# mLSTM gates as three f32r products of split parts, computed between the query/key blocks and the V projection

## Chip, core and metric

The kernel runs on one core of one Trainium2 chip. The metric is the time of one execution in microseconds (us) on the device. TensorE (PE in the profile) multiplies matrices, VectorE (DVE) and ScalarE (ACT) work on elements and may read PSUM, GpSimd (POOL) works on elements in SBUF alone, and SyncE (SP) issues most transfers from memory.

## What is computed

The reference is a network of two stacks with 512 tokens and 1024 channels: feed-forward layers, an attention layer, an mLSTM layer, and two convolutional and state-space mixers. The change lies in the mLSTM layer, which begins as follows (cut to what matters):

```python
proj = xn @ w_in                       # 1024 x (4 * 1024 + 2 * 8)
qk, v, o, gates = split(proj, [2048, 3072, 4096])
qk = silu(causal_depthwise_conv(qk, conv_w))          # width 4
q, k = split(qk, 2)
gates = gates + b_gates
i_pre, f_pre = gates[..., :8], gates[..., 8:]         # 8 heads each
...
bc = cumsum(log_sigmoid(f_pre))
m_t = maximum(bc + m_prev, max_s(bc_t - bc_s + i_s))  # running maximum
p = (q @ k.T / sqrt(128)) * exp(bc_t - bc_s + i_s - m_t)
hid = (p @ v + ...) / maximum(abs(sum(p) + ...), exp(-m_t))
```

The kernel treats all 512 tokens as one chunk, so that the running sum and the running maximum are two scans along a row of 512 for each of the 8 heads.

## The kernel before

**Split products.** The weights stream in blocks of 128 x 1024 (512 KB). A ring of four slots holds them: `raw` as loaded, `wh` the part rounded to f32r, `wl` the rest. SyncE issues the load of block b once block b-4 has been multiplied (`blocks_done`). ScalarE makes `wh` by a copy (`high_part`, L357), GpSimd makes `wl` by a subtraction (`low_part`, L365), and TensorE then runs 24 matmuls of 512 columns for the block (`block_mm`, L1624 to L1626): for each of 8 slices of the inner dimension `wh*xh`, `wl*xh` and `wh*xl`, where `xh` and `xl` are the two parts of the layer's input, split from `hf`.

**The query and key blocks** (section `mlstm.qk`, 16 blocks, numbered 0 to 15 here). `linear` takes the first three together as the input arrives (`first_three`, L1683 to L1688), then block 3, then loops over the other twelve. Each block ends in one of four PSUM banks, `lin[0]` to `lin[3]`. VectorE applies the convolution of width 4 to it in four instructions (L949 and L953), which frees the bank (`tiles_freed`), and ScalarE applies Silu into SBUF (L876). ScalarE's order in `conv_out` is fixed: Silu of tile m, then `high_part` of the block that goes in as number m+4, then Silu of tile m+1.

**The gates.** Behind the first three blocks, through the parameter `amid` of `linear`, TensorE runs `gates_tensor` (L781): 16 matmuls in plain f32, with weights of 8 columns (`wg`), into banks 4 and 5, on the unsplit input `hf`. They show as 32 records in the trace. VectorE then waits for them (`g_pe`) and runs the chain of gates in rows of 8 x 512, from L927 to L940, with ScalarE doing Abs, Exp, Ln and later Exp between its steps (L864 to L870, handed over by `g_vec` and `g_act`). All of this is written ahead of the first convolution in VectorE's order and ahead of the first Silu in ScalarE's. The convolution also writes to `hf`, which the gates' matmuls read.

**After block 15** TensorE transposes the two rows of gates (`gate_columns_tensor`, 8 small matmuls, L789 and L793) and starts the V projection (`token_major("mlstm.v")`, 8 blocks V0 to V7 in two halves of four, L1717 to L1719). A half waits until its four banks are free; ScalarE copies them out after each half (L886), behind the high parts of blocks V3 to V6. Then come the output gate (`mlstm.o`, 8 blocks) and the attention-like part over the heads, which reads the chain's results first at its start.

## Time and profile before

| what | value |
|---|---|
| median of 3 runs | 2794.43 us (2792.47 to 2794.62) |
| the profiled execution's own time | 2798.81 us |
| its span, first to last instruction | 2797.0 us |
| TensorE busy | 2591.9 us, 93% of the span |
| weight loads busy | 2081.1 us, 74% |
| GpSimd, ScalarE, VectorE busy | 1293.9, 1003.4 and 983.9 us |
| mean granted TensorE clock | 0.944 of full |

A busy time sums the time in which an engine had an instruction under way. A matmul's record is longer than its step: they overlap, so the distance between two starts is what one costs. The granted clock is the share of TensorE's full 2.4 GHz that the chip allowed in a stretch; it has two levels, 2.4 and 1.2 GHz, so that a mean between 0.5 and 1 is a mixture.

### The profile page before, as it was taken

How to read it: one execution, taken by the hardware profiler on the slowest of the kernel's cores; microseconds unless marked ns; L12 is line 12 of the kernel's file. 1: busy time of each engine (PE TensorE's matmuls, PEld its weight loads, DVE VectorE, ACT ScalarE, POOL GpSimd, SP SyncE). 2: the span in 40 equal slices, each digit the busy share in tenths (PEclk: the TensorE clock that was granted, in tenths of full speed). 3: DMA queues.
4: the chain of work that ended last, by engine and by line, in shares of the span. 5: the costliest groups of instructions: out<-in, count | busy, mean ns of one | idle time of the engine just before them, and what ended most of it. 6: DMA issues, size and time to landing. Idle time of an engine off the chain costs nothing. (4 is left out here: it accounts for less than half of the span.)

```text
span 2797.0 us, 31691 instructions
## 1 busy us (share of the span) xinstructions
PE 2591.9 (93%) x11348; PEld 2081.1 (74%) x11348; DVE 983.9 (35%) x1541; ACT 1003.4 (36%) x1351; POOL 1293.9 (46%) x683
## 2 busy tenths in 40 slices
PE   7999999899999999999999799989999986988787
PEld 5888878655788888888886676778888875766656
DVE  2222330044522211422213521634224169214973
ACT  4333333266533332433332323434333332234442
POOL 4555544300455554555543333136555453246843
PEclk9999989999999999999998899889999988998888
DMA  3233433200132333232331122022333322221211
GB/s 120 97 97 111 129 98 98 83 1 1 60 105 95 94 104 105 76 97 97 98 105 68 60 83 75 1 75 83 97 97 98 105 75 76 81 75 61 67 52 61
DMA packets 69332, 228.35 MB, mean 82 GB/s; under 512 B 8803, under 2 KB 13283, under 8 KB 69132
## 3 DMA queue, kind: packets, MB, share of 16 engines
q1 hardware_dynamic: 63456, 218.63, 24.4%
q10 hardware_dynamic: 4956, 5.61, 0.7%
q0 software_dynamic: 848, 3.15, 0.3%
q8 instruction: 46, 0.75, 0.1%
q14 instruction: 26, 0.21, 0.0%
HBM read 222.75 MB, written 6.84 MB: 82 GB/s over the span
## 5 line engine op out<-in xcount | busy, mean ns | idle before, releaser
L365 POOL TENSOR_TENSOR wl_sb<-raw_sb,wh_sb 128x1024 fp32r<-128x1024 f32 x401 | 971.2, 2425 | 1102.8 <-ACT wh_sb L357 1100.4
L1624 PE MATMUL banks<-xh_sb,wh_sb 128*128 128x512 f32 x2064 | 818.7, 397 | 77.0 <-POOL wl_sb L365 60.2
L1625 PE MATMUL banks<-xh_sb,wl_sb 128*128 128x512 f32 x2064 | 813.2, 394 | 0.0
L1626 PE MATMUL banks<-xl_sb,wh_sb 128*128 128x512 f32 x2064 | 812.5, 394 | 0.0
L357 ACT ACTIVATE wh_sb<-raw_sb 128x1024 fp32r<-128x1024 f32 x401 | 423.9, 1059 | 809.2 <-DMA raw_sb<-weights 805.6
L1624 PEld LDWEIGHTS banks<-xh_sb,wh_sb 128*128 128x128 f32 x2064 | 393.8, 191 | 168.9 <-issue 57.5
L1626 PEld LDWEIGHTS banks<-xl_sb,wh_sb 128*128 128x128 f32 x2064 | 393.6, 191 | 83.6
L1625 PEld LDWEIGHTS banks<-xh_sb,wl_sb 128*128 128x128 f32 x2064 | 394.6, 191 | 81.7
L1624 PE MATMUL banks<-hh_sb,wh_sb 128*128 128x512 f32 x704 | 273.9, 389 | 0.0
L1625 PE MATMUL banks<-hh_sb,wl_sb 128*128 128x512 f32 x704 | 273.9, 389 | 0.0
L1626 PE MATMUL banks<-hl_sb,wh_sb 128*128 128x512 f32 x704 | 273.9, 389 | 0.0
L2015 DVE TENSOR_TENSOR hf_sb<-banks,rstd_sb 128x512 f32<-128x512 f32 x88 | 60.8, 691 | 383.2 <-PE banks L1626 378.0
L2053 POOL TENSOR_TENSOR hl_sb<-hf_sb,hh_sb 128x512 f32 (+1 forms) x88 | 114.3, 1299 | 128.1 <-ACT hh_sb L1852 128.1
L394 POOL TENSOR_TENSOR xl_sb<-hf_sb,xh_sb 128x512 fp32r<-128x512 f32 x80 | 106.5, 1354 | 139.2 <-ACT xh_sb L387 91.7
L1932 DVE SCALAR_TENSOR_TENSOR xs_sb<-banks,vecs_sb,x_sb 128x512 f32<-128x512 f32 x32 | 24.0, 751 | 375.8 <-ACT hf_sb L1806 375.8
L2012 DVE TENSOR_TENSOR hf_sb<-banks,rstd_sb 128x512 f32<-128x512 f32 x88 | 60.8, 691 | 268.4 <-PE banks L1626 267.2
L1624 PEld LDWEIGHTS banks<-hh_sb,wh_sb 128*128 128x128 f32 x704 | 132.1, 188 | 27.5
L1626 PEld LDWEIGHTS banks<-hl_sb,wh_sb 128*128 128x128 f32 x704 | 132.1, 188 | 27.5
L1625 PEld LDWEIGHTS banks<-hh_sb,wl_sb 128*128 128x128 f32 x704 | 132.1, 188 | 27.3
L1852 ACT ACTIVATE hh_sb<-hf_sb 128x512 f32 (+1 forms) x88 | 55.5, 631 | 254.2 <-DVE hf_sb L2018 254.1
L1683 PE MATMUL banks<-xh_sb,wh_sb 128*128 128x512 f32 x240 | 104.8, 437 | 39.1 <-issue 24.5
L2018 DVE TENSOR_TENSOR hf_sb<-hf_sb 128x512 f32<-128x512 f32 x88 | 128.4, 1459 | 13.5 <-ACT hf_sb L1848 10.7
(357 smaller groups left out, 2706.6 us busy)
## 6 DMA issues: line engine op xcount, KB each, us to landing
raw_sb<-weights SPq DMA_DIRECT2D x404, 512.0 KB, 3.5
scratch<-scratch ACTq DMA_DIRECT2D x1, 2560.0 KB, 11.7
x_sb<-x_in SPq DMA_DIRECT2D x8, 256.0 KB, 8.7
mix_sb<-scratch POOLq DMA_DIRECT2D x1, 2048.0 KB, 9.1
out<-hf_sb SPq DMA_DIRECT2D x8, 256.0 KB, 2.2
turn<-mix_sb SPq DMA_DIRECT2D x4, 256.0 KB, 3.2
mix_sb<-turn SPq DMA_DIRECT2D x4, 256.0 KB, 4.8
turn<-mix_sb ACTq DMA_DIRECT2D x4, 256.0 KB, 2.5
```

What stands on the lines that cost most here:

```text
L357: act.activation(wh[:, slot, :], raw[:, slot, :], ACT.Copy).then_inc(w_hi, 1)
L365: pool.tensor_tensor(wl[:, slot, :], raw[:, slot, :], wh_f[:, slot, :], ALU.subtract).then_inc(w_split, 1)
L394: pool.tensor_tensor(xl[:, c, :], hf[:, c, :], xh_f[:, c, :], ALU.subtract).then_inc(xn_ready, 1)
L1624: pe.matmul(dst, wh[:, q, cols], in_hi, start=first, stop=False)
L1625: pe.matmul(dst, wl[:, q, cols], in_hi, start=False, stop=False)
L1626: return pe.matmul(dst, wh[:, q, cols], in_lo, start=False, stop=last)
L1683: pe.matmul(lin[s], wh[:, s, tile], xh[:, k, :], start=(k == 0), stop=False)
L1852: act.activation(at(hh, 2 * i + s), ht[:, s, :], ACT.Copy).then_inc(h_hi, 1)
L2012: dve.tensor_tensor(sg[:, s, :], lin[2 * s], rstd[:, :], ALU.mult).then_inc(gate_scaled, 1)
L2015: dve.tensor_tensor(ht[:, s, :], lin[2 * s + 1], rstd[:, :], ALU.mult).then_inc(tiles_freed, 2)
L2018: dve.tensor_tensor(ht[:, s, :], ht[:, s, :], sg[:, s, :], ALU.mult).then_inc(h_mul, 1)
L2053: pool.tensor_tensor(at(hl, 2 * i + s), ht[:, s, :], at(hh_f, 2 * i + s), ALU.subtract).then_inc(h_lo, 1)
```

## The change

The gates' weights are split in two parts as well. In the space of `hf` (columns 1536 to 2175, read by nobody once the input is split) two f32r tiles `gates_hi` and `gates_lo` are made, with 40 columns for each of 8 slices: input gates in columns 0 to 7, forget gates in 32 to 39, zeros between. ScalarE zeroes and fills `gates_hi` in three instructions, GpSimd `gates_lo` in three. TensorE runs three products for each slice, 24 matmuls, all into bank 4; the forget gates come out on partitions 32 to 39. The matmuls stand behind block 15 and ahead of V0, the transposes behind V7. VectorE's chain, unchanged in its instructions, stands behind the sixteen convolutions, and ScalarE's four steps of it are put behind the high parts of V3, V4 and V5.

```diff
 def gates_tensor(pe):
-    pe.wait_ge(gates_loaded, 32)
-    for g in range(2):
-        for k in range(KD):
-            last = pe.matmul(banks[0:HEADS, 4 + g, :], wg[:, 2 * HEADS * k + HEADS * g:
-                                                         2 * HEADS * k + HEADS * (g + 1)],
-                             hf[:, k, :], start=(k == 0), stop=(k == KD - 1))
+    pe.wait_ge(gates_split, 1)
+    for k in range(KD):
+        for w, v in ((gates_hi, xh), (gates_lo, xh), (gates_hi, xl)):
+            last = pe.matmul(banks[0:GATES, 4, :], w[:, GATES * k:GATES * (k + 1)], v[:, k, :],
+                             start=(k == 0 and w is gates_hi and v is xh), stop=(k == KD - 1 and v is xl))
     last.then_inc(g_pe, 1)
...
 def mlstm_scalar(act):
-    act.wait_ge(g_vec, 1)
-    act.activation(e_row, f_row, ACT.Abs).then_inc(g_act, 1)
...
+    act.wait_ge(xn_ready, SPLIT["mlstm"] + 8)
+    act.wait_ge(gates_loaded, 32)
+    act.activation(gates_hi, vec[:, 0:GATES * KD], ACT.Copy, scale=0.0).then_inc(gates_high, 1)
+    act.wait_ge(gates_high, 1)
+    given = wg[:, :].rearrange("p (k g c) -> p g k c", k=KD, g=2)
+    for g in range(2):
+        last = act.activation(both_gates(gates_hi)[g], given[:, g], ACT.Copy)
+    last.then_inc(gates_high, 1)
...
+    def gate_step(n):
+        if n == 0:
+            act.wait_ge(g_vec, 1)
+            act.activation(e_row, f_row, ACT.Abs).then_inc(g_act, 1)
+            act.wait_ge(g_act, 1)
+            act.activation(e_row, e_row, ACT.Exp, scale=-1.0).then_inc(g_act, 1)
+        elif n == 1:
+            act.wait_ge(g_act, 2)
+            act.activation(e_row, e_row, ACT.Ln, bias=1.0).then_inc(g_act, 1)
+        elif n == 2:
+            act.wait_ge(g_vec, 2)
+            act.activation(e_row, e_row, ACT.Exp, scale=-1.0).then_inc(g_act, 1)
...
         for s in range(4):
             high_part(act, "mlstm.v", s, 4 * half)
+            if half == 0:
+                gate_step(s)
...
 def mlstm_vector(dve):
-    dve.wait_ge(g_pe, 1)
-    dve.memset(one_row, 1.0)
...
     with dve.Fori(0, 4) as i:
...
+    dve.wait_ge(g_pe, 1)
+    dve.memset(one_row, 1.0)
+    link(ts(i_row, banks[0:HEADS, 4, :], vec[0:HEADS, VEC["b_i"]:VEC["b_i"] + 1], None, ALU.add))
+    ts(f_row, banks[F_ROWS, 4, :], vec[F_ROWS, VEC["b_f"]:VEC["b_f"] + 1], None,
+       ALU.add).then_inc(g_vec, 1)
+    dve.wait_ge(g_act, 3)
+    link(stt(f_row, f_row, 0.0, e_row, ALU.min, ALU.subtract))
+    link(dve.tensor_tensor_scan(cum, one_row, f_row, 0.0, ALU.mult, ALU.add))
+    tt(c_row, i_row, cum, ALU.subtract).then_inc(g_rows, 1)
+    dve.wait_ge(g_rows, 1)
+    link(dve.tensor_tensor_scan(m_row, c_row, c_row, 0.0, ALU.max, ALU.max))
+    tt(e_row, cum, m_row, ALU.add).then_inc(g_vec, 1)
+    dve.wait_ge(g_act, 4)
+    ts(e_row, e_row, 3e38, None, ALU.min).then_inc(g_cols, 1)
...
 def mlstm_pool(pool):
+            pool.wait_ge(gates_high, 2)
+            pool.tensor_tensor(gates_lo, gates_hi_f, gates_hi_f, ALU.subtract).then_inc(gates_zero, 1)
+            pool.wait_ge(gates_zero, 1)
+            for g in range(2):
+                last = pool.tensor_tensor(both_gates(gates_lo)[g], given[:, g], both_gates(gates_hi_f)[g],
+                                          ALU.subtract)
+            last.then_inc(gates_split, 1)
...
-    linear("mlstm.qk", "mlstm", gates_tensor)
+    linear("mlstm.qk", "mlstm")
+    gates_tensor(pe)
+    token_major("mlstm.v")
     gate_columns_tensor(pe)
-    token_major("mlstm.v")
```

TensorE's order around blocks 0 to 3, before (the last matmuls of the first three blocks, the gates, block 3):

```order
L1683 MATMUL banks<-xh_sb,wh_sb 128x512
L1684 MATMUL banks<-xh_sb,wl_sb 128x512
L1688 MATMUL banks<-xl_sb,wh_sb 128x512 x3
L781 MATMUL banks<-hf_sb,wg_sb 8x512 x16
L1624 MATMUL banks<-xh_sb,wh_sb 128x512
L1625 MATMUL banks<-xh_sb,wl_sb 128x512
L1626 MATMUL banks<-xl_sb,wh_sb 128x512
```

The same place of the changed kernel, whose line numbers are 37 higher there:

```order
L1720 MATMUL banks<-xh_sb,wh_sb 128x512
L1721 MATMUL banks<-xh_sb,wl_sb 128x512
L1725 MATMUL banks<-xl_sb,wh_sb 128x512 x3
L1661 MATMUL banks<-xh_sb,wh_sb 128x512
L1662 MATMUL banks<-xh_sb,wl_sb 128x512
L1663 MATMUL banks<-xl_sb,wh_sb 128x512
```

The gates have gone, and block 3 follows the first three. Behind block 15, before (loop end, transposes, V0):

```order
L1626 MATMUL banks<-xl_sb,wh_sb 128x512
L1700 REGISTER_ALU
L1700 COMPARE_AND_BRANCH
L789 MATMUL banks<-consts_sb,mix_sb 128x8 x4
L793 MATMUL banks<-consts_sb,mix_sb 128x8 x4
L1717 MATMUL banks<-wh_sb,xh_sb 128x512
```

And in the changed kernel, where the three rows of L794 stand eight times:

```order
L1663 MATMUL banks<-xl_sb,wh_sb 128x512
L1737 REGISTER_ALU
L1737 COMPARE_AND_BRANCH
L794 MATMUL banks<-xh_sb,gates_hi_sb 40x512
L794 MATMUL banks<-xh_sb,gates_lo_sb 40x512
L794 MATMUL banks<-xl_sb,gates_hi_sb 40x512
...
L1754 MATMUL banks<-wh_sb,xh_sb 128x512
```

The gates stand where the transposes stood, and nothing else is between block 15 and V0. ScalarE's order after the split of the input, before (L864 to L870 are the steps of the chain, L876 is Silu, L357 a high part):

```order
L387 ACTIVATE xh_sb<-hf_sb 128x512 x3
L864 ACTIVATE mix_sb<-mix_sb 8x512
L866 ACT_TABLE_LOAD
L866 ACTIVATE mix_sb<-mix_sb 8x512
L868 ACT_TABLE_LOAD
L868 ACTIVATE mix_sb<-mix_sb 8x512
L870 ACT_TABLE_LOAD
L870 ACTIVATE mix_sb<-mix_sb 8x512
L876 ACT_TABLE_LOAD
L876 ACTIVATE mix_sb<-hf_sb 128x512
L357 ACTIVATE wh_sb<-raw_sb 128x1024
```

The changed kernel at the same place, and then, behind the loop of convolutions, from the high part of V3 (L360 is the high part, L887 to L895 the chain's steps, L914 the copies out of the V banks):

```order
L390 ACTIVATE xh_sb<-hf_sb 128x512 x3
L877 ACTIVATE gates_hi_sb<-vecs_sb 128x320
L881 ACTIVATE gates_hi_sb<-wg_sb 128x8x8 x2
L902 ACT_TABLE_LOAD
L902 ACTIVATE mix_sb<-hf_sb 128x512
L360 ACTIVATE wh_sb<-raw_sb 128x1024
```

```order
L360 ACTIVATE wh_sb<-raw_sb 128x1024
L887 ACTIVATE mix_sb<-mix_sb 8x512
L889 ACT_TABLE_LOAD
L889 ACTIVATE mix_sb<-mix_sb 8x512
L360 ACTIVATE wh_sb<-raw_sb 128x1024
L892 ACT_TABLE_LOAD
L892 ACTIVATE mix_sb<-mix_sb 8x512
L360 ACTIVATE wh_sb<-raw_sb 128x1024
L895 ACT_TABLE_LOAD
L895 ACTIVATE mix_sb<-mix_sb 8x512
L360 ACTIVATE wh_sb<-raw_sb 128x1024
L914 ACTIVATE mix_sb<-banks 128x512 x4
```

The four steps moved from ahead of the first Silu to between the high parts of V3 to V6, and three short fills took their old place.

## Rows read from the trace of the kernel before

**Rows 1.** Waits, 1495 to 1760 us: total, times, longest.
```profile
POOL wl_sb L365 <- ACT wh_sb L357: 135.6, 32, 35.0
```

**Rows 2.** Timeline of TensorE from 1495 us: start, length, instruction, [idle <-releaser].
```profile
1528.56 0.84 PE L1688 MATMUL banks<-xl_sb,wh_sb 128*128 128x512 f32 x3
1529.33 13.90 PE L781 MATMUL banks<-hf_sb,wg_sb 128*8 128x512 f32 x32
1543.16 0.50 PE L1624 MATMUL banks<-xh_sb,wh_sb 128*128 128x512 f32 x1
```

**Rows 3.** Timeline of VectorE, 1500 to 1640 us.
```profile
1543.40 0.48 DVE L927 MEMSET mix_sb<- 8x512 f32 x1 [22.14 <-PE banks L781]
...
1544.46 0.74 DVE L929 TENSOR_SCALAR mix_sb<-banks,vecs_sb 8x512 f32<-8x512 f32 x1
1549.78 0.68 DVE L932 SCALAR_TENSOR_TENSOR mix_sb<-mix_sb 8x512 f32<-8x512 f32 x1 [4.58 <-ACT mix_sb L868]
...
1555.50 0.75 DVE L949 TENSOR_SCALAR hf_sb<-banks,vecs_sb 128x512 f32<-128x512 f32 x1
```

**Rows 4.** Timeline of ScalarE, 1500 to 1640 us.
```profile
1545.24 0.63 ACT L864 ACTIVATE mix_sb<-mix_sb 8x512 f32<-8x512 f32 x1 [23.31 <-DVE mix_sb L929]
...
1547.83 1.28 ACT L868 ACT_TABLE_LOAD   x1
...
1554.42 0.63 ACT L870 ACTIVATE mix_sb<-mix_sb 8x512 f32<-8x512 f32 x1 [3.37 <-DVE mix_sb L937]
```

**Rows 5.** Timeline of GpSimd, 1515 to 1570 us.
```profile
1521.85 3.79 POOL L394 TENSOR_TENSOR xl_sb<-hf_sb,xh_sb 128x512 fp32r<-128x512 f32 x3
1560.65 2.35 POOL L365 TENSOR_TENSOR wl_sb<-raw_sb,wh_sb 128x1024 fp32r<-128x1024 f32 x1 [35.01 <-ACT wh_sb L357]
```

**Rows 6.** Timeline of TensorE from 1560 us, blocks 4 to 10.
```profile
1563.14 0.79 PE L1624 MATMUL banks<-xh_sb,wh_sb 128*128 128x512 f32 x1 [14.24 <-POOL wl_sb L365]
...
1569.16 0.40 PE L1626 MATMUL banks<-xl_sb,wh_sb 128*128 128x512 f32 x1
...
1599.12 0.39 PE L1626 MATMUL banks<-xl_sb,wh_sb 128*128 128x512 f32 x1
```

**Rows 7.** Loads of the tile raw, 1528 to 1545 us, on SP's queue.
```profile
L1640 SPq DMA_DIRECT2D raw_sb<-weights x3: 332/333/333, 1529.1 to 1530.3; - x3
...
DMA to landing us min/median/max: 3.5/4.2/5.5
```

**Rows 8.** Timeline of TensorE from 1630 us, start of the V projection.
```profile
1631.40 0.41 PE L789 MATMUL banks<-consts_sb,mix_sb 8*128 8x8 f32 x4
...
1635.19 0.80 PE L1717 MATMUL banks<-wh_sb,xh_sb 128*128 128x512 f32 x1 [3.13 <-DVE hf_sb L953]
...
1641.04 0.39 PE L1719 MATMUL banks<-wh_sb,xl_sb 128*128 128x512 f32 x1
```

**Rows 9.** Timeline of ScalarE in the V projection.
```profile
1647.05 1.06 ACT L357 ACTIVATE wh_sb<-raw_sb 128x1024 fp32r<-128x1024 f32 x1 [10.21 <-DMA raw_sb<-weights]
...
1658.16 1.06 ACT L357 ACTIVATE wh_sb<-raw_sb 128x1024 fp32r<-128x1024 f32 x1 [4.50 <-DMA raw_sb<-weights]
1659.85 2.07 ACT L886 ACTIVATE mix_sb<-banks 128x512 f32<-128x512 f32 x4 [0.63 <-PE banks L1719]
```

**Rows 10.** Timeline of TensorE behind three other idles.
```profile
433.68 0.49 PE L1624 MATMUL banks<-xh_sb,wh_sb 128*128 128x512 f32 x1 [1.57 <-POOL wl_sb L365]
...
524.14 0.50 PE L1717 MATMUL banks<-wh_sb,xh_sb 128*128 128x512 f32 x1 [2.15 <-ACT mix_sb L549]
...
1661.96 0.50 PE L1717 MATMUL banks<-wh_sb,xh_sb 128*128 128x512 f32 x1 [2.15 <-ACT mix_sb L886]
```

**Rows 11.** Windows of TensorE: length, busy (x), granted clock, DMA share, GB/s.
```profile
524.00:528.00 4.00, 3.86 (x10) 0.57 0.24 93
1662.00:1668.00 6.00, 6.00 (x27) 1.00 0.14 58
```

**Rows 12.** The page's costliest groups: the gated product of the feed-forward layer.
```profile
L2018 DVE TENSOR_TENSOR hf_sb<-hf_sb 128x512 f32<-128x512 f32 x88 | 128.4, 1459 | 13.5 <-ACT hf_sb L1848 10.7
```

More of the change, by code:

```diff
@@ L222, in build @@
         gates_loaded = sem("gates_loaded")
+        gates_high = sem("gates_high")
+        gates_split = sem("gates_split")
+        gates_zero = sem("gates_zero")
         h_mul = sem("h_mul")
@@ L775, in build, with both_gates @@
         diag_m = [hf[:, 6 + e, :] for e in range(2)]
-        def gates_tensor(pe):
-            pe.wait_ge(gates_loaded, 32)
-            for g in range(2):
-                for k in range(KD):
-                    last = pe.matmul(banks[0:HEADS, 4 + g, :], wg[:, 2 * HEADS * k + HEADS * g:
-                                                                 2 * HEADS * k + HEADS * (g + 1)],
-                                     hf[:, k, :], start=(k == 0), stop=(k == KD - 1))
+        F_ROWS = slice(32, 32 + HEADS)
+        GATES = 32 + HEADS
+        gates_hi, gates_lo = (place(n, HF + 1536 + GATES * KD * j, GATES * KD, F32R)[:, :]
+                              for j, n in enumerate(("gates_hi", "gates_lo")))
+        gates_hi_f = gates_hi.bitcast(F32)
+        def both_gates(buf):
+            wide = buf.rearrange("p (k c) -> p k c", k=KD)
+            return wide[:, :, 0:HEADS], wide[:, :, F_ROWS]
+        def gates_tensor(pe):
+            pe.wait_ge(gates_split, 1)
[3 more added lines that the diff above has]
+                                     start=(k == 0 and w is gates_hi and v is xh), stop=(k == KD - 1 and v is xl))
             last.then_inc(g_pe, 1)
@@ L862, in mlstm_scalar @@
         def mlstm_scalar(act):
-            act.wait_ge(g_vec, 1)
-            act.activation(e_row, f_row, ACT.Abs).then_inc(g_act, 1)
-            act.wait_ge(g_act, 1)
-            act.activation(e_row, e_row, ACT.Exp, scale=-1.0).then_inc(g_act, 1)
-            act.wait_ge(g_act, 2)
-            act.activation(e_row, e_row, ACT.Ln, bias=1.0).then_inc(g_act, 1)
-            act.wait_ge(g_vec, 2)
-            act.activation(e_row, e_row, ACT.Exp, scale=-1.0).then_inc(g_act, 1)
+            act.wait_ge(xn_ready, SPLIT["mlstm"] + 8)
[18 more added lines that the diff above has]
+                    act.activation(e_row, e_row, ACT.Exp, scale=-1.0).then_inc(g_act, 1)
             def conv_out(i):
@@ L924, in link @@
                 dve.wait_ge(g_chain, chain[0])
-            dve.wait_ge(g_pe, 1)
-            dve.memset(one_row, 1.0)
-            link(ts(i_row, banks[0:HEADS, 4, :], vec[0:HEADS, VEC["b_i"]:VEC["b_i"] + 1], None, ALU.add))
-            ts(f_row, banks[0:HEADS, 5, :], vec[0:HEADS, VEC["b_f"]:VEC["b_f"] + 1], None,
-               ALU.add).then_inc(g_vec, 1)
-            dve.wait_ge(g_act, 3)
-            link(stt(f_row, f_row, 0.0, e_row, ALU.min, ALU.subtract))
-            link(dve.tensor_tensor_scan(cum, one_row, f_row, 0.0, ALU.mult, ALU.add))
-            tt(c_row, i_row, cum, ALU.subtract).then_inc(g_rows, 1)
-            dve.wait_ge(g_rows, 1)
-            link(dve.tensor_tensor_scan(m_row, c_row, c_row, 0.0, ALU.max, ALU.max))
-            tt(e_row, cum, m_row, ALU.add).then_inc(g_vec, 1)
-            dve.wait_ge(g_act, 4)
-            ts(e_row, e_row, 3e38, None, ALU.min).then_inc(g_cols, 1)
             mc = VEC["mconv_w"]
@@ L1031, in mlstm_pool @@
             for name in ("mlstm.qk", "mlstm.v", "mlstm.o"):
+                if name == "mlstm.qk":
+                    pool.wait_ge(gates_high, 2)
+                    pool.tensor_tensor(gates_lo, gates_hi_f, gates_hi_f, ALU.subtract).then_inc(gates_zero, 1)
+                    pool.wait_ge(gates_zero, 1)
+                    given = wg[:, :].rearrange("p (k g c) -> p g k c", k=KD, g=2)
+                    for g in range(2):
+                        last = pool.tensor_tensor(both_gates(gates_lo)[g], given[:, g], both_gates(gates_hi_f)[g],
+                                                  ALU.subtract)
+                    last.then_inc(gates_split, 1)
                 low_parts(pool, name, name == "mlstm.qk")
@@ L2220 @@
     vecs[0:HEADS, VEC["b_i"]] = a["mlstm_b_gates"][0, 0:HEADS]
-    vecs[0:HEADS, VEC["b_f"]] = a["mlstm_b_gates"][0, HEADS:]
+    vecs[32:32 + HEADS, VEC["b_f"]] = a["mlstm_b_gates"][0, HEADS:]
     def diagonal(v):
```

## Prediction

> **What bounds the kernel now.** I began with the busy times: TensorE has an instruction under way 93% of the span, so a change pays only where it lets TensorE stand still less, run fewer steps or keep its clock. The view of waits for the first part of the mLSTM layer shows where it stands still: the longest wait of GpSimd there, for a high part from ScalarE, is 35.0 us [rows 1]. The timelines follow that chain around the place that the change touches.
>
> TensorE finishes blocks 0 to 2 at about 1529.0 to 1529.4, runs the gates in f32 for 13.9 us and starts block 3 at 1543.16 [rows 2]. VectorE has waited 22.14 us for the gates and begins its chain at 1543.40; the first convolution, of a block done since 1529, starts at 1555.50 [rows 3]. Only then come its Silu, the high part of block 4 behind that Silu, the low part (1560.65 on GpSimd, [rows 5]) and TensorE at 1563.14, after 14.24 us of idling [rows 6]. So from 1529.33 to 1563.14 TensorE does one block and the gates. Two more losses hang on it. It restarts at half clock: from 1563.14 to 1569.16 it starts 14 matmuls at about 0.43 us each, where the full clock has 29.96 us for the 132 from 1569.16 to 1599.12, or 0.227 each [rows 6]. And behind block 15 it does the transposes at 1631.40, waits 3.13 us for the last convolution and again begins V0 at half clock, 14 steps in 5.85 us [rows 8].
>
> **The part around blocks 0 to 4.** Removed from TensorE's path are 33.81 us (1529.33 to 1563.14) in which it now has block 3 alone. After the change block 3 runs from 1529.33 for 24 x 0.227 = 5.4 us and ends at 1534.8. Block 4 waits for the chain that begins with the first convolution. SyncE's first load there is issued at 1529.1, on the same signal (block 0 done) that releases VectorE [rows 7], so I start the convolution at 1529.2. From its start to TensorE's start on block 4 the chain took 1563.14 - 1555.50 = 7.64 us before [rows 3, 6]; all its members are kept. Block 4 then starts at 1529.2 + 7.64 = 1536.84, 26.3 us earlier.
>
> The load of block 4 must have landed when its high part begins. A high part takes 1.06 us [rows 9] and ran just ahead of the low part's 1560.65 [rows 5], so it began about 4.0 us into the chain; now that is 1533.2. The three loads land 3.5, 4.2 and 5.5 us after issue [rows 7]; if they finish in their order, block 4 is there at 1532.6, 0.6 us early. Attention has the same section without a convolution in it, and TensorE idled 1.57 us ahead of its block 4, for the low part [rows 10]; 1.9 to 2.0 us here, with a slightly longer chain, fits that.
>
> Added at this place are the fills. ScalarE now waits for GpSimd's last low part of the input, 1521.85 + 3.79 = 1525.64 [rows 5]; nothing is queued behind it until the first Silu at 1532.7. Three copies of at most 320 columns, each bounded by the 0.63 us of a row of 512 [rows 4], and one table load of 1.28 end before 1529. GpSimd's three subtractions, each bounded by the 1.26 us of a 128x512 one [rows 5], end before 1532; its next work is the low part of block 4 at 1534.3. Lower bound for all six: nothing. I take nothing, since 2 to 3 us of cover remain on both engines; without it they would delay block 4 one for one, up to 5.7 us in sum. The new wait of TensorE on `gates_split` has the whole V projection behind it, but is met 70 us ahead.
>
> **The clock at block 4.** After 1.9 us of idling the clock may stay or fall. Two idles of 2.15 us tell both stories [rows 10]: after one the next 4 us had a granted clock of 0.57, after the other 6 us had 1.00 [rows 11]. A fall after such an idle costs (4 us at 0.57) 1.4 to 1.7 us. Bounds are 0 and the 2.85 us of the restart at 1563.14 (6.02 us for 14 steps, against 3.17). I take 0: it is nearest to the 1.57 us case, behind which the first matmul's record had its short length, 0.49 us against 0.79 at 1563.14 [rows 6, 10].
>
> **Blocks 4 to 15.** From block 4's start to the transposes it was 1631.40 - 1563.14 = 68.26 us [rows 6, 8]; less 2.85 of cold start it is 65.4. With the convolutions running beside them these blocks kept 0.227 us a step without a pause from 1569.16 to 1599.12 [rows 6], though they began with VectorE further behind than it will be now; so nothing else holds this stretch. Block 15 ends at 1536.84 + 65.4 = 1602.2.
>
> **The gates' new place.** 24 matmuls with 40 columns of weights. No row has an f32r matmul with so few columns. Near rows: the 128-column f32r step of 0.227, and the gates' f32 records of 8 columns, 13.90/32 = 0.434 each, two per matmul, so 0.87 for a matmul of 512 in f32 [rows 2]. If only the dtype counts it is 24 x 0.227 = 5.4 us; at f32's pace 20.9 us. I take 5.4, since in the two rows of 128-column weights and of 8-column ones a step of 512 moving columns costs a whole fraction of each other (0.227 and 0.217 times two or four), whatever the weights' width. V0 can start at 1602.2 + 5.4 + 0.2 (the step from loop to straight code, 1631.40 against the last start) = 1607.8. The last convolution, which held V0 for 3.13 us, is over 3.9 us after block 15 and lies under the gates. V0 started at 1635.19: 27.4 us earlier. Without an idle ahead of it V0 keeps its clock: 5.85 - 14 x 0.227 = 2.7 us more.
>
> "TensorE: Matmul & The Clock Gate" of the Trainium skill, section "Back-to-back issue gap", has N/2.4 + 2.5 ns between warm matmuls, 216 ns for 512 columns, whatever the weights. Its "LDWEIGHTS" section gives 40 columns a third of the load of 128. By it the 24 matmuls would cost 5.2 us, 0.3 less than by the trace's 0.227; the trace's slower step is with full-width weights, so this case could lie at either.
>
> **The chain under the V projection.** Shift V's rows by 30.1 us. Behind the gates (end 1607.9) VectorE delivers the forget row 1545.24 - 1543.40 = 1.84 us after it starts [rows 3, 4], at 1609.9. Abs, load and Exp take 2.59 us (to the Ln's load) [rows 4]: 1612.5, before the high part of V4 at 1647.05 - 30.1 = 1616.9 [rows 9]. Ln, behind it, with 1.06, 1.28 and 0.63, ends at 1619.9. VectorE's next steps took 1549.78 to 1554.38, 4.6 us [rows 3, 4]: 1624.5, Exp ends at 1625.2. The next high part, V6, waits for its load until 1658.16 - 30.1 = 1628.1 anyway [rows 9]. So all steps lie inside waits for loads, with 2.9 us to spare at the tightest; each us beyond, and beyond the 0.63 that ScalarE then waits for TensorE [rows 9], would delay the copies out of the banks and V4. GpSimd is at work in V and was idle during the old chain, and that counts: where it works, a VectorE product with both inputs in SBUF takes 1459 ns [rows 12] and the chain's steps of 512 take 0.68 [rows 3]. Were all five steps held by 0.8 us, the chain would be 4.0 us longer and V4 0.5 late. GpSimd works 2.4 us [rows 5] of each block's 5.4, so I take 0. The transposes, now behind V7, fall into TensorE's idle while ScalarE copies the second half.
>
> "GPSIMD Engine Reference" of the Trainium skill, section "Key points", says that the engines contend when a VectorE instruction has two SBUF inputs. The trace agrees, 1459 ns against 0.68 us, and by the rule alone, all five steps held, the gain would be 0.5 us smaller.
>
> **The sum.** 27.4 + 2.7 = 30.1 us. The profiled execution took 2798.81 us, 4.4 above the median of the runs; it would take 2768.7, and the median goes from 2794.43 to 2764.3.
>
> **Rivals.** (a) The clock falls once or twice at the shortened idles, block 4 and then V4 or the output gate, whose idles of 2.15 us and more happened to keep it: 1.5 to 3 us dearer, 2765.8 to 2767.3. For it: the idle at 524.14. (b) Loads finish together instead of in order, at 5.5 us: the high part of block 4 begins at 1534.8 to 1535.7, 1.6 to 2.5 late, the idle passes 3 us and the clock falls as it did behind 3.13 [rows 8], 2.85: 2769.2. Against it: the spread 3.5, 4.2, 5.5. (c) Narrow f32r weights run at f32's pace: 15.5 us dearer, 2779.8. Against it: no sign in the rows. (d) The chain is stretched by GpSimd far beyond 0.8 us a step, with the evacuation late: up to 4 us, 2768. (e) Slower than before: if the convolution let only one block at a time go through, so that a block could not start before the chain of the one before had ended, each of twelve blocks would cost 5.4 + 7.64 = 13 us, +91 us, near 2855; it turns the change into a loss once a block's cycle passes 5.4 + 30.1/12 = 7.9 us. Four banks and the 0.227 us pace through blocks 4 to 10 [rows 6] speak against it. (f) The change frees nothing because block 4 waits on something else until 1563: 2794. Only loads and the first Silu remain, both long done.
>
> **How the numbers follow.** Forecast 0.60, with its own range 2762.5 to 2766; (a) 0.25, (b) 0.05, (c) 0.03, (d) 0.04, (e) 0.01, (f) 0.02. The range runs from 2761.5 (narrow weights at 0.217, a share of cold starts elsewhere gone) to 2769.5, which leaves out (c), (e), (f) and the tails. 0.2% of the time, 5.6 us, is about what a measurement can tell from no change. Faster by more than that: 0.97; within: 0.02; slower: 0.01.
>
> **What would show it.** TensorE: block 3 at 1529, an idle near 2 us, then no idle until V4; 24 matmuls with 40 columns in 5.2 to 5.5 us; no idle and no half clock at V0. ScalarE: high parts of V4 to V6 still released by loads. VectorE: first convolution 0.2 us behind block 0. The prediction fails if the idle at block 4 is above 3 us, the 24 matmuls take over 6 us, or the high part of V6 waits for Exp.

## The result

| | before | changed |
|---|---|---|
| median of 4 runs each | 2794.52 us (2792.47 to 2795.91) | 2773.01 us (2770.21 to 2775.20) |
| profiled execution, its own time | 2798.81 us | 2770.21 us |
| its span, mean granted clock | 2797.0 us, 0.944 | 2768.3 us, 0.948 |

The ratio is 0.9923, 95% interval 0.9906 to 0.9940. The change makes the kernel 21.5 us faster, not 30.1; 2773.0 lies 3.5 us above the stated range. The two profiled executions, one of each, are 28.6 us apart: the sum's own figure for the changed one, 2768.7 us, was missed by 1.5 us.

TensorE's timeline of the changed kernel at the places of [rows 2, 6, 8], with the last matmuls of the first three blocks, block 3, block 4, the first and last of the gates and V0:

```profile
1528.90 0.84 PE L1725 MATMUL banks<-xl_sb,wh_sb 128*128 128x512 f32 x3
1529.58 0.39 PE L1661 MATMUL banks<-xh_sb,wh_sb 128*128 128x512 f32 x1
...
1537.21 0.49 PE L1661 MATMUL banks<-xh_sb,wh_sb 128*128 128x512 f32 x1 [2.03 <-POOL wl_sb L368]
```

```profile
1602.64 0.40 PE L794 MATMUL banks<-xh_sb,gates_hi_sb 128*40 128x512 f32 x1
...
1607.96 0.39 PE L794 MATMUL banks<-xl_sb,gates_hi_sb 128*40 128x512 f32 x1
1608.19 0.40 PE L1754 MATMUL banks<-wh_sb,xh_sb 128*128 128x512 f32 x1
```

Block 3 follows the first three blocks at once, block 4 waits 2.03 us, the gates' 24 steps take 1608.19 - 1602.64 = 5.55 us, and V0 has no idle in front of it. VectorE, ScalarE and GpSimd around blocks 0 to 4, the answers to [rows 3 to 5]:

```profile
1529.56 0.75 DVE L961 TENSOR_SCALAR hf_sb<-banks,vecs_sb 128x512 f32<-128x512 f32 x1 [9.41 <-PE banks L1725]
```

```profile
1524.57 0.47 ACT L877 ACTIVATE gates_hi_sb<-vecs_sb 128x320 fp32r<-128x320 f32 x1 [3.75 <-POOL xl_sb L397]
...
1525.49 1.28 ACT L902 ACT_TABLE_LOAD   x1
1533.06 0.63 ACT L902 ACTIVATE mix_sb<-hf_sb 128x512 f32<-128x512 f32 x1 [6.28 <-DVE hf_sb L965]
1533.60 1.05 ACT L360 ACTIVATE wh_sb<-raw_sb 128x1024 fp32r<-128x1024 f32 x1
```

```profile
1525.55 0.72 POOL L1062 TENSOR_TENSOR gates_lo_sb<-gates_hi_sb 128x320 fp32r<-128x320 f32 x1 [1.02 <-ACT gates_hi_sb L881]
1526.35 0.60 POOL L1066 TENSOR_TENSOR gates_lo_sb<-wg_sb,gates_hi_sb 128x64 fp32r<-128x64 f32 x2
1534.72 2.35 POOL L368 TENSOR_TENSOR wl_sb<-raw_sb,wh_sb 128x1024 fp32r<-128x1024 f32 x1 [7.77 <-ACT wh_sb L360]
```

The first convolution starts at 1529.56 instead of 1555.50. The fills of ScalarE and GpSimd end at 1527, far ahead of the first Silu and the low part of block 4. The chain under the V projection, on ScalarE (the answer to [rows 9]) and on VectorE:

```profile
1610.36 0.63 ACT L887 ACTIVATE mix_sb<-mix_sb 8x512 f32<-8x512 f32 x1 [2.17 <-DVE mix_sb L970]
...
1617.55 1.06 ACT L360 ACTIVATE wh_sb<-raw_sb 128x1024 fp32r<-128x1024 f32 x1 [4.61 <-DMA raw_sb<-weights]
...
1619.92 0.63 ACT L892 ACTIVATE mix_sb<-mix_sb 8x512 f32<-8x512 f32 x1
1622.83 1.06 ACT L360 ACTIVATE wh_sb<-raw_sb 128x1024 fp32r<-128x1024 f32 x1 [2.28 <-DMA raw_sb<-weights]
...
1627.61 0.63 ACT L895 ACTIVATE mix_sb<-mix_sb 8x512 f32<-8x512 f32 x1 [2.41 <-DVE mix_sb L978]
1628.26 1.06 ACT L360 ACTIVATE wh_sb<-raw_sb 128x1024 fp32r<-128x1024 f32 x1
1630.17 2.06 ACT L914 ACTIVATE mix_sb<-banks 128x512 f32<-128x512 f32 x4 [0.84 <-PE banks L1756]
```

```profile
1620.59 1.04 DVE L973 SCALAR_TENSOR_TENSOR mix_sb<-mix_sb 8x512 f32<-8x512 f32 x1 [10.26 <-ACT mix_sb L892]
...
1624.87 2.70 DVE L978 TENSOR_TENSOR mix_sb<-mix_sb 8x512 f32<-8x512 f32 x1
```

GpSimd's subtractions in that stretch:

```profile
1618.69 2.40 POOL L368 TENSOR_TENSOR wl_sb<-raw_sb,wh_sb 128x1024 fp32r<-128x1024 f32 x1 [8.03 <-ACT wh_sb L360]
1623.97 3.06 POOL L368 TENSOR_TENSOR wl_sb<-raw_sb,wh_sb 128x1024 fp32r<-128x1024 f32 x1 [2.89 <-ACT wh_sb L360]
```

Two of VectorE's steps are held: 1.04 and 2.70 us instead of 0.68. Both start while GpSimd is at work and both end 0.54 us after its subtraction does (1621.09 to 1621.63, 1627.03 to 1627.57). The chain's last Exp comes out at 1628.24 and the high part of V6 follows it without an idle, where the forecast had 2.9 us to spare. The load of V6 landed at 1628.24 too, so the high part was no later than its load would have allowed, and ScalarE still waits 0.84 us for TensorE ahead of the copies.

What the page and these rows do not show is seen only when whole stretches are laid beside each other. The starts are read from TensorE's timelines; "before" and "changed" have several profiled executions, all of them listed:

| stretch, us | before (2) | changed (3) |
|---|---|---|
| first matmul of block 0 to last x3 group of block 2 | 17.12, 18.53 | 18.57, 17.08, 17.07 |
| from there to V0 | 106.63, 105.75 | 79.29, 80.91, 80.93 |
| V0 to V4 | 26.77, 25.83 | 24.10, 24.10, 24.09 |
| V4 to the output gate | 24.49, 24.48 | 26.07, 26.07, 26.07 |
| output gate to the heads | 46.71, 46.69 | 48.25, 48.31, 48.19 |
| heads to the output projection | 97.73, 97.74 | 93.26, 93.31, 90.07 |
| state-space layer, first matmul to the first group with `xl` (L1688, L1725) of its output projection | 187.08, 185.02 | 190.67, 190.26, 190.60 |
| the same group of the last output projection to the last group of matmuls | 50.90, 50.81 | 51.08, 50.81, 51.04 |

From block 0 to V0 it is 123.75 and 124.28 us before and 97.86, 97.99 and 98.00 after, so 25.8 to 26.4 us less, and 1.7 to 2.7 less from there to V4: nearly the forecast. Behind it, in code that it does not touch, stretches grow by 1.6, 1.6 and some 4.5 us (3.2 to 5.7), one shrinks by 4.4 or 7.7 and the last keeps its 51 us. For the first two the windows over the idles ahead of V4 and the output gate say why. For the second profile of before and the second and third of the changed kernel (length, busy and count, granted clock, DMA):

```profile
1661.00:1665.00 4.00, 3.86 (x17) 1.00 0.25 101
1685.00:1689.00 4.00, 3.38 (x15) 1.00 0.27 111
```

```profile
1632.00:1636.00 4.00, 3.95 (x10) 0.57 0.24 99
1658.00:1662.00 4.00, 3.88 (x12) 0.69 0.19 76
```

```profile
1632.00:1636.00 4.00, 3.26 (x8) 0.62 0.35 122
1658.00:1662.00 4.00, 3.19 (x10) 0.78 0.30 119
```

The idle ahead of V4 is 2.15 us in all of them, the one ahead of the output gate 2.43 before and 1.83 after the change. Behind the same or a shorter idle the clock is half for a while in the changed kernel and full in the one before.

The length of the heads follows the clock too. The whole stretch in the first profile of before, in the third of the changed kernel and in the experiment `filled_parted` below:

```profile
1733.16:1830.89 97.73, 91.08 (x432) 0.81 0.00 1
1707.00:1797.07 90.07, 83.58 (x432) 0.88 0.01 2
1702.54:1806.23 103.69, 97.80 (x432) 0.76 0.00 1
```

The same 432 matmuls take 90 to 104 us, the less the higher their mean granted clock (0.88, 0.81, 0.76).

### The profile page after: what moved, and what is told of

The parts are those of the page before. It is cut to its first block and busy times, and to the rows that moved or that the text cites. A ratio compares the mean times of both kernels' runs of the same rounds, so it can differ in the third digit from the quotient of the medians.

```text
span 2768.3 us, 31682 instructions
## 1 busy us (share of the span) xinstructions
PE 2577.2 (93%) x11340; PEld 2079.1 (75%) x11340; DVE 985.2 (36%) x1541; ACT 1004.2 (36%) x1354; POOL 1296.0 (47%) x686
## 5 line engine op out<-in xcount | busy, mean ns | idle before, releaser
L360 ACT ACTIVATE wh_sb<-raw_sb 128x1024 fp32r<-128x1024 f32 x401 | 423.9, 1059 | 802.3 <-DMA raw_sb<-weights 798.5
L1661 PEld LDWEIGHTS banks<-hh_sb,wh_sb 128*128 128x128 f32 x704 | 132.1, 188 | 27.3
```

The source lines that it names most:

```text
L360: act.activation(wh[:, slot, :], raw[:, slot, :], ACT.Copy).then_inc(w_hi, 1)
L1661: pe.matmul(dst, wh[:, q, cols], in_hi, start=first, stop=False)
```

## Experiments

**Both kernels again.** No edit.

> The kernel before, unchanged, to learn how much two executions differ. If the 30.1 us of the sum are right and the missing 8 us are luck of single executions and of the chip, then this profile is several us shorter than the first one (2798.8), and its shorter time lies outside the part from the first three blocks to V0, which stays at 105.9 us (1529.33 to 1635.19). If instead the sum is wrong, the profile repeats 2798.8 within 1 us. Time ratio to the kernel before: 1.000 within 0.001.

> The changed kernel, unchanged, on the same chip as the kernel before. Theory one (the sum is right, the first comparison was between chips or lucky executions): 28 to 30 us shorter, ratio near 0.9896. Theory two (part is given back behind V0 in most executions, by the clock after the idles at V4 and the output gate, or in the heads): 21 to 25 us shorter, ratio 0.991 to 0.9925, with the stretch from the first three blocks to V0 at 78.5 us all the same.

> The changed kernel once more, beside the three that follow. Its times have spread over 9 us (2768.0 to 2776.7) where those of before spread over 6. 22 to 25 us shorter than before; half clock behind the V4 and output-gate idles in this profile if that is the usual way, as in the two profiles so far (26.07 and 48.3 us), not if it is chance.

Measured: before 2794.59 us (ratio 1.0004, 0.9995 to 1.0012), its profiled execution 2794.66. Changed 2770.38 (0.9920, 0.9907 to 0.9933) and 2771.31 (0.9918, 0.9905 to 0.9932). The profile that the prediction was worked out from was a long execution: 2798.81, where the 11 of this repeat lie between 2792.77 and 2798.60. Those 4.1 us lie elsewhere than the change: it is 0.5 us shorter than the repeat from the layer's first block to V0, but 0.9 us longer from there to V4, 2.1 in the state-space layer, 0.7 behind it, 0.5 in the stretch ahead of it and 0.4 ahead of the mLSTM layer. The real difference is 23 to 24 us by these two runs, 21.5 by the first, so theory one falls: the sum is short of something in most executions. The half clock at V4 and the output gate is in three profiles of three of the changed kernel.

**The kind of product and the place, apart.** The first keeps f32 gates, without the fills, and takes the new place; the convolutions get buffers of their own there, since the f32 gates still read the input that lies in the old ones. The second has the f32r gates at the old place, with the chains ahead of the convolutions.

```diff
 # f32_late (cut: the fills taken out, the forget row read from bank 5)
-    for w, v in ((gates_hi, xh), (gates_lo, xh), (gates_hi, xl)):
-        last = pe.matmul(banks[0:GATES, 4, :], w[:, GATES * k:GATES * (k + 1)], v[:, k, :],
+        last = pe.matmul(banks[0:HEADS, 4 + g, :], wg[:, 2 * HEADS * k + HEADS * g:
+                                                     2 * HEADS * k + HEADS * (g + 1)],
+                         hf[:, k, :], start=(k == 0), stop=(k == KD - 1))
...
+conv_buf = [region(22784 + T * j, T) for j in range(2)]
...
-c = cbuf[m % 2]
+c = conv_buf[m % 2]
 # f32r_early (cut: the chains of VectorE and ScalarE, moved ahead of the convolutions)
-linear("mlstm.qk", "mlstm")
-gates_tensor(pe)
+linear("mlstm.qk", "mlstm", gates_tensor)
+gate_columns_tensor(pe)
 token_major("mlstm.v")
-gate_columns_tensor(pe)
```

> The gates as 16 plain f32 matmuls as before, but at the new place behind block 15, with the chain under V; the convolution's two buffers lie elsewhere, since the gates read hf. The sum says: 13.9 us of matmuls instead of 5.6, so 8.3 us longer than the changed kernel and 19 to 22 us shorter than before. A rival (the kind of product is what pays, the place is free) would have it no better than 5 us under before.

> The gates as 24 f32r matmuls with 40 columns, but at the old place behind the first three blocks, with VectorE's and ScalarE's chain ahead of the convolutions as before. The sum says: only 13.9 - 5.5 = 8.4 us shorter than before, with the idle of 14 us ahead of block 4 still there and the half clock behind it. If the place were worth little it would come within 5 us of the changed kernel.

Measured: `f32_late` 2777.61 us, ratio 0.9949 (0.9937 to 0.9961); `f32r_early` 2789.98, 0.9982 (0.9973 to 0.9991). TensorE in the one and the other:

```profile
1603.29 13.90 PE L795 MATMUL banks<-hf_sb,wg_sb 128*8 128x512 f32 x32
1617.12 0.50 PE L1738 MATMUL banks<-wh_sb,xh_sb 128*128 128x512 f32 x1
```

```profile
1530.74 0.40 PE L794 MATMUL banks<-xh_sb,gates_hi_sb 128*40 128x512 f32 x1
...
1556.38 0.79 PE L1662 MATMUL banks<-xh_sb,wh_sb 128*128 128x512 f32 x1 [14.47 <-POOL wl_sb L368]
```

The late f32 gates take 1617.12 - 1603.29 = 13.8 us against 5.55, so the product is worth 8.3 us, and the whole is 7.2 us longer than the repeat of the changed kernel and 16.8 us shorter than before, where 19 to 22 was expected; the rival, no more than 5 us under before, falls. With the f32r gates at the old place the idle of 14.47 us ahead of block 4 is as before [rows 6]. Its stretch to V0 is 98.15 us, 7.6 to 8.5 less than before, as forecast, but the median gains only 4.4 us, where 8.4 was expected. So the place is the larger part, by either way of taking the change apart (16.8 of 24 us, or 19.6), and here too some 4 us are missing. Its one profile, 6.4 us shorter than the repeat of before, does not show where.

**The transposes ahead of V0.**

```diff
+for n in range(3):
+    gate_step(n)
...
-        if half == 0:
-            gate_step(s)
...
+gate_columns_tensor(pe)
 token_major("mlstm.v")
-gate_columns_tensor(pe)
```

> The changed kernel with the two rows of gates transposed ahead of V0 instead of behind V7, and ScalarE's four steps of the chain ahead of the high part of V3: TensorE waits for the whole chain. By the rows of before the chain from the gates' end is 0.2 + 1.84 + 2.59 + 1.9 + 4.6 + 0.7 + 0.5, or about 12.3 us, plus 0.7 for the transposes, and V0 restarts at half clock for 1.7 to 2.8 us: V0 begins 13 us later and the kernel is 14 to 16 us longer than the changed one, so 8 to 10 us shorter than before. If the place of the chain did not matter it would stay within 2 us of the changed kernel.

Measured: 2784.39 us, ratio 0.9958 (0.9945 to 0.9971). TensorE waits for the chain twice, once for each row of gates:

```profile
1618.88 0.59 PE L801 MATMUL banks<-consts_sb,mix_sb 8*128 8x8 f32 x4 [9.24 <-DVE mix_sb L975]
1621.95 0.59 PE L805 MATMUL banks<-consts_sb,mix_sb 8*128 8x8 f32 x4 [2.48 <-DVE mix_sb L981]
```

The stretch to V0 is 93.90 us, 13.0 to 14.6 more, and V0 restarts at half clock (26.36 to V4 instead of 24.10). The total is 13 us longer than the changed kernel's, 1 less than expected, which shows that it is the wait for the chain that costs: here the idles at V4 and the output gate kept the clock (24.49 and 46.66).

**Idle work added.** Matmuls whose result nobody reads, 128x512 in f32r, 0.23 us each. They change no value that is used.

```diff
+def pad(pe, n):
+    for _ in range(n):
+        pe.matmul(banks[:, 5, :], xh[:, 0, 0:P], xh[:, 0, :], start=True, stop=True)
 # pad_v5
 gates_tensor(pe)
+pad(pe, 5)
 token_major("mlstm.v")
 # pad_f10, and pad_f5 with 5, in ffn()
+if idx == 3:
+    pad(pe, 10)
 pe.wait_ge(h_lo, 2 + KF * idx + 16)
```

> The changed kernel with 5 idle matmuls (f32r, 128x512, result unused) between the gates and V0: 1.15 us of extra TensorE work, which moves everything behind it later by that much. If the part that was given back behind V0 is a matter of when TensorE's idles fall against the chip's clock decisions, the V4 and output-gate idles (half clock behind both in both profiles of the changed kernel) should keep the clock, as before the change: V4 to output gate back from 26.07 to 24.5 us and output gate to heads from 48.3 to 46.7, the heads perhaps back from 93.3 to 97.7; in sum about as long as the changed kernel, within 3 us either way. If it is not a matter of timing, every stretch keeps its length and the kernel is 1.15 us longer.

> The changed kernel with 10 idle matmuls (2.3 us) inside the fourth feed-forward layer, behind its gate and up blocks: all up to there is untouched, the state-space layer starts 2.3 us later. Theory clock timing: the stretch even to evenout (187.6 and 188.0 us in the changed kernel, 182.3 to 184.4 in four others) falls to 182 to 185, and the last stretch from 52.5 to 51: in sum 1 to 4 us shorter than the changed kernel although it does more. Rival (the change itself makes the later layer slower, through addresses, transfers or the tables that ScalarE loads): the stretch stays at 188 and the kernel is 2.3 us longer.

> 5 idle matmuls (1.15 us) in the fourth feed-forward layer, half of the 10 that made the kernel 3 us shorter. If the state-space layer's length is decided by the clock behind its block 4 and the order of transfers there, it comes out either long (190 to 191 us from its first matmul to the next layer's) or short (185 to 187), with nothing between the two and no relation to the 1.15 us added; the total then is either 2 us longer than the changed kernel or 2 to 3 us shorter. If extra work simply adds up: 1.15 us longer.

Measured: `pad_v5` 2768.15 us, ratio 0.9902 (0.9889 to 0.9915); `pad_f10` 2767.96, 0.9903 (0.9890 to 0.9916); `pad_f5` 2772.08, 0.9923 (0.9909 to 0.9936). Two kernels that do more work came out 3 us shorter than the changed one; the intervals overlap, so what is shown is that they are not longer by what they add. In `pad_v5` V4 to the output gate is 24.48 us and the granted clock is full:

```profile
1635.00:1639.00 4.00, 3.94 (x17) 1.00 0.20 78
```

The state-space layer is 186.87 us in `pad_f10` and 189.33 in `pad_f5`. The second refutes my "long or short, nothing between". The 52.5 us that the expectation of `pad_f10` names for the last stretch were a misreading: that stretch is 50.8 to 51.1 us in the kernel before and in the changed one, so nothing was to be won there. `pad_f10` and `pad_f5` carry a warning too: their V projection is the changed kernel's, instruction for instruction, and has 24.48 and 46.7 us in it. `after_even` below, again with the same instructions up to there, is a third such case:

```profile
1631.00:1635.00 4.00, 4.00 (x19) 1.00 0.14 55
```

So of six profiles with the same V projection behind the same idle of 2.15 us, three have the half clock and three have not: it is frequent, but not a fixed property of the code.

**The gates parted.**

```diff
-def gates_tensor(pe):
+def gates_tensor(pe, part=(3, KD)):
...
-    for k in range(KD):
+    for k in range(*part):
...
-linear("mlstm.qk", "mlstm")
+linear("mlstm.qk", "mlstm", behind=lambda pe: gates_tensor(pe, (0, 3)))
```

> The changed kernel with the gates' 24 matmuls parted: 9 of them (slices 0 to 2) between block 3 and block 4, where TensorE idled 2.03 us, and 15 behind block 15. Local sum: block 4 starts at most 0.2 us later, the second part is 2.1 us shorter, V0 then waits for the last convolution until 3.9 us behind block 15 instead of 5.6: 1.5 us earlier. In total 1.5 us shorter than the changed kernel if the rest kept its length; with the rest moving by the clock, anything from 4 us shorter to 2 us longer.

Measured: 2772.00 us, ratio 0.9917 (0.9902 to 0.9932). The stretch to V0 is 77.65 us, 1.6 less than 79.29, as the local sum had it; the median does not show it. V4 and the output gate are at 26.08 and 48.35, the state-space layer at 190.69.

**Idles filled.** The same idle matmuls, placed where TensorE waits anyway.

```diff
 # filled
 for half in range(2):
+    if half and name == "mlstm.v":
+        pad(pe, 9)
     pe.wait_ge(tiles_freed, FREE0 + TILE[name] + 4 * half)
...
 gate_columns_tensor(pe)
+pad(pe, 7)
 pe.wait_ge(tiles_freed, FREE0 + TILE["mlstm.o"])
 # filled_parted: the same on top of the parted gates
```

> The changed kernel with idle matmuls placed into two idles of TensorE: 9 ahead of V4's wait (2.1 us into an idle of 2.15 and the step before it) and 7 ahead of the output gate's (1.6 us into 1.83). Theory clock: they cost nothing, since TensorE waits there for ScalarE's copies anyway, and the clock stays full: V4 to output gate 24.5 us, output gate to heads 46.7 us, together 3.1 us less than in the changed kernel's profiles; what the heads give back by the clock in turn may be up to 4.4. Rival (the two stretches are long for another reason than the idle's clock): 26.07 and 48.3 us stay.

> The last one and the parted gates (9 matmuls between block 3 and block 4) together. Theory: the first three blocks' end to V4 as in the parted kernel, 101.9 us, then 24.5 and 46.7 us: 4 to 5 us less than the changed kernel up to the heads. In total 2766 to 2769 if the state-space layer is long, 2762 to 2765 if short; the best version so far.

Measured: `filled` 2769.54 us, ratio 0.9915 (0.9901 to 0.9928); `filled_parted` 2770.64, 0.9907 (0.9892 to 0.9923). TensorE at V4 in `filled`, and the clock over both places:

```profile
1629.02 0.39 PE L1762 MATMUL banks<-wh_sb,xl_sb 128*128 128x512 f32 x1
1629.25 2.20 PE L792 MATMUL banks<-xh_sb 128*128 128x512 f32 x9
1631.57 0.50 PE L1760 MATMUL banks<-wh_sb,xh_sb 128*128 128x512 f32 x1
```

```profile
1631.00:1635.00 4.00, 3.88 (x17) 1.00 0.32 112
1656.00:1660.00 4.00, 4.00 (x18) 1.00 0.16 66
```

V4 starts 2.55 us after the last matmul of V3, as it did with the idle (1632.29 - 1629.75 in the changed kernel): the nine cost nothing. The two stretches are 24.53 and 46.73 us, in `filled_parted` 24.51 and 46.67. At full clock they have their old lengths, so the 3.1 us are the clock's, and the rival falls. That the fills kept the clock full is not shown: it was full in all three filled profiles (`filled_even` is the third), but also in three of the six unfilled ones. The heads took the 3.1 us back: 97.54 us in `filled` and 103.70 in `filled_parted`, where the changed kernel had 90 to 93. The mean clock of `filled_parted` was 0.76 there. It was expected at 2769 us or less, as the best version so far, and was not. No filled version is clearly faster than the changed kernel.

**The state-space layer.** Its input projection is split like the query and key blocks, and TensorE idles ahead of its block 4 too.

```diff
 def dense(m):
+    if m == 4:
+        pad(pe, 8)
     pe.wait_ge(w_split, BLK[name] + m + 1)
```

> The kernel before with 8 idle matmuls (1.8 us) ahead of block 4 of the state-space layer's input projection, where TensorE idles 2.0 to 3.0 us. Theory clock: the layer (first matmul to the next layer's) is 184 to 187 us, as it was or up to 2 us shorter; total 0 to 2 us shorter than before. Rival: 1.8 us longer.

> The changed kernel with the same 8 idle matmuls there, where it idles 3.3 to 3.5 us. Theory clock: the clock stays full behind the idle, the wait of 0.6 to 1.9 us for the transfer of the turned tensor goes, and the layer is 184 to 187 us instead of 190.5, the same as in the filled kernel before; the total is 4 to 5 us shorter than the changed kernel's 2771, and 26 to 28 us shorter than the filled kernel before. Rival (the change makes the layer longer by itself): the layer stays at 190 us or more, and the two filled kernels stay 23 us apart.

> The changed kernel with idle matmuls at all three places, V4, output gate and block 4 of the state-space layer: 24.5, 46.7 and 184 to 187 us in the three stretches. Total 2763 to 2768, close to the forecast of 2764.3, if the heads are at 93 to 98 us.

Measured: `before_even` 2796.18 us, ratio 1.0007 (0.9998 to 1.0016); `after_even` 2768.13, 0.9911 (0.9897 to 0.9924); `filled_even`, on top of `filled`, 2769.10, 0.9919 (0.9906 to 0.9933). The layer is 185.83, 186.64 and 185.01 us. TensorE and its clock behind block 4's start in the third profile of the changed kernel and in `after_even`:

```profile
2263.11 0.50 PE L1661 MATMUL banks<-xh_sb,wh_sb 128*128 128x512 f32 x1 [3.34 <-POOL wl_sb L368]
...
2286.53 3.70 PE L1206 MATMUL banks<-mix_sb 128*128 128x128 f32 x31 [1.63 <-DMA mix_sb<-turn]
```

```profile
2263.00:2271.00 8.00, 7.89 (x31) 0.79 0.00 1
```

```profile
2267.20 0.50 PE L1667 MATMUL banks<-xh_sb,wh_sb 128*128 128x512 f32 x1 [1.43 <-POOL wl_sb L368]
```

```profile
2267.00:2275.00 8.00, 7.80 (x42) 1.00 0.13 24
```

Unfilled, the clock falls behind an idle of 3.34 us, and later TensorE waits 1.63 us for the transfer of the turned tensor; filled, neither happens. From block 4 to the matmuls behind that wait it is 22.4 to 23.7 us in the three profiles of the changed kernel and 20.0 in `after_even`. But it is 20.0 in `pad_v5` as well, which kept the clock behind an idle of 3.08 us without a fill. So these 2.4 to 3.7 us go with the clock and the late transfer, and that the fill saved them is not shown.

Nor are they all. Block 4 starts 25.5 or 27.8 us behind the layer's first matmul, with nothing between, in nine and eight of the seventeen profiles: 27.80 and 25.48 in the two of before, 27.8 in all three of the changed kernel. `pad_f10` (25.6) and `pad_f5` (27.8) have the same instructions there, and show what decides. VectorE's product and GpSimd's low part of block 4, for which TensorE waits, in the one and the other:

```profile
2259.87 4.45 DVE L1162 TENSOR_TENSOR mix_sb<-gain_sb,mix_sb 128x2048 f32<-128x2048 f32 x1
```

```profile
2259.79 2.37 POOL L368 TENSOR_TENSOR wl_sb<-raw_sb,wh_sb 128x1024 fp32r<-128x1024 f32 x1 [8.96 <-ACT wh_sb L360]
```

```profile
2264.48 2.29 DVE L1162 TENSOR_TENSOR mix_sb<-gain_sb,mix_sb 128x2048 f32<-128x2048 f32 x1
```

```profile
2264.52 4.47 POOL L368 TENSOR_TENSOR wl_sb<-raw_sb,wh_sb 128x1024 fp32r<-128x1024 f32 x1 [9.07 <-ACT wh_sb L360]
```

The two start within 0.1 us of each other, and the second takes 2.1 to 2.2 us longer than when it comes first. If that is GpSimd's, block 4 is late by as much. No experiment moved this order on purpose.

With the same edit in both, the kernels lie 28.0 us apart by their medians (2796.18 and 2768.13, each against runs of before with the median 2793.81), where without it they lay 21.5 to 24 apart. The clock theory had 26 to 28, the rival 23. This does not decide between them: 2.4 of the 28.0 us come from `before_even` being longer than before, where 0 to 2 us shorter was expected, and the intervals, some 2.5 and 3.8 us to each side, do not exclude 23. `after_even` is 2.9 us shorter than the 2771 of its expectation instead of 4 to 5; its heads took 99.56 us, at a mean clock of 0.79. `filled_even` is above its 2763 to 2768.

## Why the prediction was wrong

**The waits and the path: right.** Block 4 was forecast 7.5 us behind the release of block 3 (1529.33 to 1536.84) and came 7.6 behind it (1529.58 to 1537.21). Its idle was forecast at 1.9 to 2.0 us and was 2.03. Blocks 4 to 15 were forecast at 65.4 us and took 1602.64 - 1537.21 = 65.4. The step that bears most was right: removing the gates' chain from ahead of the first convolution is the larger part of the change.

**The gates' matmuls: right.** 5.4 us forecast, 5.55 measured, at 0.23 us a step, so not at f32's pace. It is 0.4 us more than the 5.2 us that the prediction worked out from "TensorE: Matmul & The Clock Gate" of the Trainium skill, section "Back-to-back issue gap". That section gives its 216 ns as the gap of an isolated matmul and says that in a stream the weight loads count too, so "whatever the weights" was more than it states. Here a step took 0.231 us with 40 columns of weights and 0.227 with 128: narrow weights gained nothing.

**V0: right, but for the clock.** 27.4 us earlier relative to the end of the first blocks was forecast; 106.63 - 79.29 = 27.3 in the first pair of profiles. Measured from block 0's start it is 123.75 - 97.86 = 25.9, because the first blocks themselves took 1.45 us longer there. The 2.7 us of V0's clock are the 26.77 to 24.10 of the table.

**The chain under V: right in its effect, wrong in its margin.** I forecast 4.6 us for VectorE's five steps and took 0 for GpSimd. They took 7.0 us (1620.59 to 1627.57), 2.4 more, of which 2.0 in one step. That is far more than the 0.8 us a step that I had weighed, since a step that meets GpSimd's subtraction lasts until 0.54 us behind its end; in sum it stays below the 4.0 us of that weighing. The spare 2.9 us covered it: Exp ended at 1628.24, when V6's load landed. That nothing was lost by it was close.

**The clock at block 4: a value taken at its best bound.** I took 0. It was 0 in the first profile (stretch 79.29 us) and 1.6 us in the two others (80.91, 80.93). The three are alike all the same: where block 4 kept the clock, block 0 had restarted with the longer stretch at half clock (18.57 us for the first blocks against 17.07). So some 1.5 us were lost at one of the two places in each of the three (`pad_f10`, with the same instructions, lost them at neither: 17.28 and 79.28 us), as the windows behind block 0's and block 4's starts show, for the first and the second profile:

```profile
1513.00:1517.00 4.00, 4.00 (x12) 0.58 0.00 0
1537.00:1541.00 4.00, 3.79 (x17) 1.00 0.26 100
```

```profile
1513.00:1517.00 4.00, 4.00 (x19) 1.00 0.00 0
1537.00:1541.00 4.00, 4.00 (x13) 0.62 0.00 0
```

**The sum: this is the step that failed.** It took everything behind V0 as unchanged, a term of nothing without a reason, and the time before as a constant from which a local gain can be subtracted. Rival (a) named one mechanism, the clock at block 4, V4 or the output gate, with 1.5 to 3 us and a chance of 0.25. In the three profiles of the changed kernel it was the usual case and larger: 1.5 us at block 0 or 4 in each, 1.6 at V4 and 1.6 at the output gate in three of three. A place that I did not name at all, the state-space layer 600 us later, cost about 4.5 us more, in part by the order of VectorE and GpSimd ahead of its block 4, in part by the clock and a transfer that then came late. The heads, which I did not name either, gave back 4.4 at a higher clock. From the second profile of before to the second of the changed kernel the account is: 1.1 us already ahead of the layer, 26.3 from block 0 to V0, 1.7 to V4, then -1.6, -1.6, +4.4 and -5.2, with -0.4 in small terms, in sum 24.7 us against the 30.1 of the forecast. So 2.1 us of the forecast are missing up to V4 and 4.4 behind it with the small terms, less the 1.1 that came from ahead.

In the first pair the same places gave 28.6 us, close to 30.1, and that was luck: 1.1 us came from ahead of the layer, and 25.9 and 2.7 up to V4 were followed by -1.6, -1.5, +4.5 and -3.6, with +1.1 in small terms. That profile of before was also longer than all the timed executions of before in the first comparison and in its repeat.

The traces show that the half clock makes the two stretches at V4 and the output gate long, and the length of the heads goes with it. Why it falls in one execution and not in another no experiment settled: it was full in three profiles of three with the fills and in three of six without.

**The range was too narrow.** Its upper end lay 5.2 us above the forecast; three places with some 1.5 us each and one with 4.5, less the heads' 4.4, come to 4.6 and nearly fill it. Single executions of one kernel spread over 6 us (before, 11 of them) and 9 us (changed, 5) here, which alone should have widened it.

**What stays open.** Why the changed kernel's V projection loses its clock so often while `pad_f10`, `pad_f5` and `after_even`, with the same instructions up to there, kept it in their profiles. Why GpSimd's low part comes first or second in the state-space layer. One profile for each kernel cannot give the share of executions. `f32r_early` lost some 4 us of its 8 in a way that no profile of it shows. And whether a version can keep these 3 to 5 us for good was not found: `pad_v5`, `pad_f10` and `after_even` have medians of 2768.0 to 2768.2 against 2770.4 to 2773.0, with intervals that overlap.

## What to carry to other kernels

When a small chain on VectorE and ScalarE stands ahead of the work that feeds TensorE, moving the chain under a stretch where those engines only wait for loads is worth far more than making its matmuls cheaper: 17 to 20 us here, against 7 (4 where it stood alone). Price such a move locally with confidence, but do not carry the local sum to the total unreduced: every idle of 1.8 to 3.5 us behind the moved place may or may not cost its 1.6 us of clock, in either kernel, so add the count of such idles to the range. To see whether a lost stretch is the clock's, lay its length beside its granted clock in several profiles of the same instructions. Filling the idle ahead of it with matmuls that nobody reads cost nothing here, but one filled profile proves little, since the clock also stays full by itself.
